# The two ends of a two-model forward pass: inputs in another order, first chunk in halves, last product by token tile

## The reference

```python
for l in range(2):                                   # first block
    proj = rms_norm(h, g_mix[l]) @ w_in[l]            # q, k, v, xr, gr
    o = diff_attention(rope(q), rope(k), v, lam)      # 4 heads of 2 x 64, causal
    y = rg_lru(causal_conv(xr), ...) * gelu(gr)       # lru_lambda -> softplus factors
    h = h + concat([o, y]) @ w_out[l]
    h = h + square(relu(rms_norm(h, g_mlp[l]) @ w_mlp_in[l])) @ w_mlp_out[l]
    gate = sigmoid(rms_norm(h, g_ple[l]) @ w_ple_gate[l])
    h = h + gate * (p[l] @ w_ple_proj[l])
h = rms_norm(h, g_final)
for i in range(4):                                   # second block
    h = h + 0.5 * swiglu(rms_norm(h, norm_ffn1[i]), ...)
    h = h + mixer[i](rms_norm(h, norm_mix[i]))        # stick-breaking, moba, mla, stick-breaking
    h = h + 0.5 * swiglu(rms_norm(h, norm_ffn2[i]), ...)
return rms_norm(h, final_norm)
```

## Time and profile before

| | us |
|---|---|
| median of 3 runs (lowest, highest) | 2667.62 (2664.0, 2668.47) |
| the profiled execution | 2668.11 |
| its span | 2666.3 |
| PE busy | 2598.2 (97%) |
| PE weight loads busy | 2237.3 (84%) |
| DVE busy | 1696.3 (64%) |
| ACT busy | 1348.9 (51%) |
| POOL busy | 57.3 (2%) |

### The profile page before, as it was taken

The page is one execution under the profiler, slowest core; times in us unless marked ns, Lnnn a source line. Parts: engine busy times, 40 slices in busy tenths (PEclk is TensorE's granted clock), DMA queues, the critical chain, the costliest instruction groups (busy, mean ns, idle before and its releaser), DMA issues.

```text
span 2666.3 us, 38170 instructions
## 1 busy us (share of the span) xinstructions
PE 2598.2 (97%) x14918; PEld 2237.3 (84%) x14918; DVE 1696.3 (64%) x1856; ACT 1348.9 (51%) x1593; POOL 57.3 (2%) x27
## 2 busy tenths in 40 slices
PE   7999999999999999999999999999999999999998
PEld 7788887887888988888888888888878888898887
DVE  7665576655766666666666666666756666665765
ACT  6644465445544454454444544544654454454543
POOL 0000000000000000000000000000000000000000
PEclk9999999999999999999999999999999999999999
DMA  7355543554455335545543455555335555543551
GB/s 274 111 195 192 187 146 116 203 189 178 174 189 180 136 130 200 190 174 190 190 157 127 158 189 189 175 190 187 127 131 192 189 176 190 190 154 111 190 189 63
DMA packets 63352, 454.36 MB, mean 170 GB/s; under 512 B 7072, under 2 KB 7328, under 8 KB 8720
## 3 DMA queue, kind: packets, MB, share of 16 engines
q1 hardware_dynamic: 61920, 448.82, 47.2%
q0 software_dynamic: 896, 3.05, 0.3%
q10 hardware_dynamic: 432, 1.00, 0.1%
HBM read 451.79 MB, written 1.05 MB: 170 GB/s over the span
## 4 chain that ended last, share of the span: by engine, by line
PE 90%; DVE 4%; ACT 4%; issue 1%; DMA 1%; SPq 0%; DVEq 0%; ACTq 0%
PE tb L484 24%; PE tb L482 14%; PE acc L269 10%; PE acc L271 9%; PE acc L270 9%; PE tb L481 3%; PE acc L235 2%; PE acc L237 2%; PE acc L238 2%; DVE w_lo L208 1%; PE acc L783 1%; PE tb L300 1%; PE acc L784 1%; PE acc L785 1%; ACT w_hi L201 1%
## 5 line engine op out<-in xcount | busy, mean ns | idle before, releaser
L208 DVE TENSOR_TENSOR w_lo<-raw,w_hi 128x2048 fp32r<-128x2048 f32 x417 | 955.0, 2293 | 323.4 <-ACT w_hi L201 322.7
L484 PE MATMUL tb<-xT,w_hi 128*128 128x512 f32 x2772 | 987.8, 396 | 0.0
L201 ACT ACTIVATE w_hi<-raw 128x2048 fp32r<-128x2048 f32 x426 | 814.2, 1912 | 323.4 <-PE acc L271 279.2
L482 PE MATMUL tb<-xT,w_lo 128*128 128x256 f32 x3168 | 818.4, 279 | 0.0
L482 PEld LDWEIGHTS tb<-xT,w_lo 128*128 128x128 f32 x3168 | 597.0, 188 | 33.8
L484 PEld LDWEIGHTS tb<-xT,w_hi 128*128 128x128 f32 x2772 | 520.2, 188 | 107.0
L269 PE MATMUL acc<-w_hi,cat 128*128 128x512 f32 x1024 | 403.6, 394 | 11.4 <-DVE cat L1865 7.8
L271 PE MATMUL acc<-w_lo,cat 128*128 128x512 f32 x1024 | 399.9, 391 | 0.0
L270 PE MATMUL acc<-w_hi,cat 128*128 128x512 f32 x1024 | 399.7, 390 | 0.0
L269 PEld LDWEIGHTS acc<-w_hi,cat 128*128 128x128 f32 x1024 | 193.0, 188 | 50.8 <-DVE cat L1865 8.7
L271 PEld LDWEIGHTS acc<-w_lo,cat 128*128 128x128 f32 x1024 | 193.0, 188 | 41.1
(11 more groups left out here) (337 smaller groups left out, 3080.0 us busy)
## 6 DMA issues: line engine op xcount, KB each, us to landing
raw<-in_stream SPq DMA_DIRECT2D x426, 1024.0 KB, 4.8
h<-in_x SPq DMA_DIRECT2D x2, 512.0 KB, 4.6
gain<-in_gains POOLq DMA_DIRECT2D x2, 512.0 KB, 9.4
xn<-in_gates POOLq DMA_DIRECT2D x2, 512.0 KB, 8.1
out<-xn SPq DMA_DIRECT2D x2, 512.0 KB, 2.7
cst<-in_consts ACTq DMA_DIRECT2D x1, 832.5 KB, 12.3
big<-in_pT POOLq DMA_DIRECT2D x2, 256.0 KB, 5.5
big<-in_lam_qk POOLq DMA_DIRECT2D x1, 256.0 KB, 10.7
```

The lines of the kernel that those rows point to most:

```text
L201: act.activation(w_hi[:, k % SPLIT, :], raw[:, k % RAW, :], ACT.Copy).then_inc(hi_done, 1)
L208: dve.tensor_tensor(w_lo[:, k % SPLIT, :], raw[:, k % RAW, :], w_hi[:, k % SPLIT, :], ALU.subtract).then_inc(lo_done, 1)
L482: last = pe.matmul(banks[f][:, 0:SEQ], lo, xT[:, kt, 0, :], start=False, stop=False)
L484: last = pe.matmul(banks[f], hi, both, start=False, stop=kt == KT - 1)
```

## The change

**Loads.** The identity now has the column of frequencies beside it (129 columns); the other constants go from ACT's queue to SP's, behind chunk 1. Chunk 0 comes as two halves. POOL's queue brings the positions first, and `lru_par` and `lam_qk` after chunk 1 has landed; the `gain` load stands at the second ple phase. **First chunk.** ACT and DVE split chunk 0 in halves between the pieces of `xT`; PE starts X0 after the first half. Chunk 3 is split before the norm's factor. `start_dve` is divided in `start_angles` (after the remainder of chunk 1), `start_dots` and `start_factors` (ahead of the rotary tables); `start_act` moves behind `rb` and chunk 4. **Spread.** The spread of the factor stands in G0, at step 8 in layer 0 and 2 in layer 1, and not at step 7 of X1. **Gated projections.** The table and the four sigmoids stand ahead of the last weight copy. **End.** The last product finishes token tile 0 first, the factor is made for each tile, POOL multiplies by the gain, and ACT and DVE apply the factor. Shapes and sums are else the same.

```diff
+        def half_hi(act, j):
+
+            act.wait_ge(*(when("half_in", 0) if j == 0 else (raw_full[0], 16)))
+            p = slice(j * HALF, (j + 1) * HALF)
+            act.activation(w_hi[:, 0, p], raw[:, 0, p], ACT.Copy).then_inc(*(sig("half_hi", 0) if j == 0 else (hi_done, 1)))
+
+        def half_lo(dve, j):
+            dve.wait_ge(*(when("half_hi", 0) if j == 0 else (hi_done, 1)))
+            p = slice(j * HALF, (j + 1) * HALF)
+            dve.tensor_tensor(w_lo[:, 0, p], raw[:, 0, p], w_hi[:, 0, p],
+                              ALU.subtract).then_inc(*(sig("half_lo", 0) if j == 0 else (lo_done, 1)))
...
-            pe.wait_ge(lo_done, c + 1 + RAW * i)
+            if c == 0:
+                pe.wait_ge(*when("half_lo", 0))
+            else:
+                pe.wait_ge(lo_done, c + 1 + RAW * i)
...
-            elif acc_done is not None:
+            elif acc_done is not None and not by_tile:
...
+                if kt == KT // 2 and n == 0:
+                    pe.wait_ge(lo_done, 1)
...
-            residual(dve, n, c + CHUNKS_FFN - 1, row_scale)
+            if f < 2 * DEPTH_B - 1:
+                residual(dve, n, c + CHUNKS_FFN - 1, row_scale)
+            else:
+                end_dve(dve, n, c + CHUNKS_FFN - 1)
+
+        END = N_NORMS - 1
...
+        def end_dve(dve, n, c_last):
+
+            def add(t, nn):
+                if (t, nn) == (1, 1):
+                    used(dve, c_last)
+                else:
+                    dve.wait_ge(*when("acc_done", (c_last, t, nn)))
...
+            add(0, 0)
+            add(0, 1)
+            add(1, 0)
+            mean(0)
+            add(1, 1)
+            factor(0)
+            mean(1)
+            factor(1)
+            dve.wait_ge(*when("end_gained", (1, 0)))
+            dve.tensor_scalar(xn[:, 1, 0:512], xn[:, 1, 0:512], e_rstd[:, 1:2], None, ALU.mult).then_inc(*sig("end_half", 0))
+
+        def end_act(act):
+            for t in range(TT):
+                for nn in range(2):
+                    h_ready(act, END, t, nn)
+                    part = slice(nn * 512, (nn + 1) * 512)
+                    last = act.activation(cut(D * t + 512 * nn, 512), h[:, t, part], ACT.Square,
+                                          accum_out=e_ss[:, 2 * t + nn:2 * t + nn + 1])
+                last.then_inc(*sig("sumsq", (END, t)))
+                if t == 0:
+                    act.preload_act_table_set("sqrt_and_others")
+                act.wait_ge(*when("meansq", (END, t)))
+                act.activation(e_rms[:, t:t + 1], e_ms[:, t:t + 1], ACT.Sqrt).then_inc(*sig("root", (END, t)))
+            for t in range(TT):
+                act.wait_ge(*when("end_rstd", t))
+                act.wait_ge(*when("end_gained", (t, 1)))
+                part = slice(0, D) if t == 0 else slice(512, D)
+                act.activation(xn[:, t, part], xn[:, t, part], ACT.Copy, scale=e_rstd[:, t:t + 1])\
+                   .then_inc(*sig("normed", (t, 1)))
+
+        def end_pool(pool):
+            pool.wait_ge(*when("gain_in", END))
+            for t in range(TT):
+                for nn in range(2):
+                    part = slice(nn * 512, (nn + 1) * 512)
+                    h_ready(pool, END, t, nn)
+                    pool.tensor_tensor(xn[:, t, part], h[:, t, part], gain[:, part], ALU.mult).then_inc(*sig("end_gained", (t, nn)))
...
-            for j in range(4):
+            for j in range(3):
                 split_hi(act, c, j + SPLIT)
+            act.preload_act_table_set("sigmoid_and_others")
...
+            split_hi(act, c, 3 + SPLIT)
...
-            product(X1, {7: lambda: spread(pe, n)})
-            product(G0)
+            product(X1)
+            product(G0, {8 if l == 0 else 2: lambda: spread(pe, n)})
...
-            split_hi(act, c, X0 + SPLIT)
+            if l:
+                split_hi(act, c, X0 + SPLIT)
             spread_act(act, n, "mix_a")
             split_hi(act, c, X1 + SPLIT)
+            if l == 0:
+                start_act(act)
             split_hi(act, c, G0 + SPLIT)
...
+            act.wait_ge(*when("factors", 0))
...
-            split_lo(dve, c, X0 + SPLIT)
+            if l:
+                split_lo(dve, c, X0 + SPLIT)
...
+            if l == 0:
+                start_factors(dve)
+                dve.wait_ge(*when("sines", 0))
             dve.tensor_tensor(rb_cos, rb, ropeA[:, 0, :], ALU.mult)
...
+        def start_dots(dve):
+            own = in_turn(dve, "dots")
+            dve.wait_ge(*when("start_in", 1))
             dve.wait_ge(*when("gain_T_in", 0))
...
+        def start_angles(dve):
+            own = in_turn(dve, "angles")
+            dve.wait_ge(*when("places_in", 0))
+            dve.wait_ge(*when("ident_in", 0))
...
-            for k in range(RAW):
+            sp.dma_start(raw[:, 0, 0:HALF], stream[0, :, 0:HALF]).then_inc(*sig("half_in", 0, 16))
+            sp.dma_start(raw[:, 0, HALF:CH], stream[0, :, HALF:CH]).then_inc(raw_full[0], 16)
+            load(1, 1)
+            sp.dma_start(cst[:, C_ROT:C_END], consts[:, C_ROT:C_END]).then_inc(*sig("const_in", 0, 16))
+            for k in range(2, RAW):
...
-                sp.wait_ge(*when("normed", (N_NORMS - 1, t)))
+                sp.wait_ge(*when("normed", (t, 1)))
+                if t:
+                    sp.wait_ge(*when("end_half", 0))
...
+            pool.dma_start(ropeA[:, 1, :].bitcast(mybir.dt.int32), positions.partition_broadcast(P)).then_inc(*sig("places_in", 0, 16))
+            pool.wait_ge(raw_full[1], 16)
             pool.dma_start(lru_par[:, :, :], lru_cols).then_inc(*sig("start_in", 0, 16))
-            pool.dma_start(ropeA[:, 1, :].bitcast(mybir.dt.int32), positions.partition_broadcast(P)).then_inc(*sig("start_in", 1, 16))
-            pool.dma_start(cut(0, 512), lam_qk.partition_broadcast(P)).then_inc(*sig("start_in", 2, 16))
-            pool.dma_start(gain[:, :], gains[0, :].partition_broadcast(P)).then_inc(*sig("gain_in", BRIDGE, 16))
+            pool.dma_start(cut(0, 512), lam_qk.partition_broadcast(P)).then_inc(*sig("start_in", 1, 16))
...
+                    if l == DEPTH_A - 1:
+                        pool.dma_start(gain[:, :], gains[0, :].partition_broadcast(P)).then_inc(*sig("gain_in", BRIDGE, 16))
...
+                if kind == "end":
+                    end_pool(pool)
...
-            act.dma_start(cst[:, 0:P], consts[:, 0:P]).then_inc(*sig("ident_in", 0, 16))
+            act.dma_start(cst[:, 0:C_ROT], consts[:, 0:C_ROT]).then_inc(*sig("ident_in", 0, 16))
             act.dma_start(gain_T[:, :, :], gains_T).then_inc(*sig("gain_T_in", 0, 16))
-            act.dma_start(cst[:, P:C_END], consts[:, P:C_END]).then_inc(*sig("const_in", 0, 16))
+            act.preload_act_table_set("sqrt_and_others")
             act.wait_ge(*when("gain_T_in", 0))
             last_kind = None
             for kind, l, c, n in PHASES:
+                if n == 0:
+                    x_high(act, n, 0)
+                    half_hi(act, 0)
+                    x_high(act, n, 1)
+                    x_high(act, n, 2)
+                    half_hi(act, 1)
+                    x_high(act, n, 3)
+                    for k in range(1, SPLIT + 1):
+                        split_hi(act, k)
+                elif kind != "end":
+                    norm_act(act, n)
+                    split_hi(act, c, -1 + SPLIT)
                 if kind != "end":
-                    norm_act(act, n)
-                if n == 0:
-                    for k in range(SPLIT):
-                        split_hi(act, k)
-                else:
-                    split_hi(act, c, -1 + SPLIT)
-                factor_act(act, n)
-                if n == 0:
-                    start_act(act)
+                    factor_act(act, n)
                 if kind not in ("ffn", "mla", "mix_a"):
                     spread_act(act, n, kind)
                 if kind != "end":
                     MIX[kind][1](act, l, c, n)
+                else:
+                    end_act(act)
...
-                    norm_dve(dve, n, last_kind)
                 if n == 0:
-                    for k in range(SPLIT):
-                        split_lo(dve, k)
+                    x_low(dve, n, 0)
+                    half_lo(dve, 0)
+                    x_low(dve, n, 1)
+                    x_low(dve, n, 2)
+                    half_lo(dve, 1)
+                    x_low(dve, n, 3)
+                    split_lo(dve, 1)
+                    start_angles(dve)
+                    split_lo(dve, 2)
+                    split_lo(dve, 3)
...
-                    start_dve(dve)
+                    start_dots(dve)
```

73 lines of the change are left out of this document (44 added, 29 removed).

## The result

| | before | after |
|---|---|---|
| median, us | 2668.05 (2664.0 to 2669.29, 4 runs) | 2649.18 (2645.5 to 2651.33, 4 runs) |
| profiled execution, us | 2668.11 | 2648.8 |
| its span, us | 2666.3 | 2647.0 |

The ratio is 0.9931, 95% interval 0.9919 to 0.9942: 18.9 us less, where 20.0 had been summed up.

What follows compares the result with a forecast made beforehand. TensorE was taken to bound the kernel, with 90% of the chain, so only its waits, low clock and two ends could be won. Start 9.0, spread 0.9, gated projections 7.8 and end 2.3 sum to 20.0: 2647.6 us, range 2643 to 2653.

Steps and rivals of the forecast that it cites:

- Start, 9.0 predicted: Start of the kernel: scores at 53.5 instead of 62.95, 9.5 us, less 0.5 for the exponentials; ends 7 and 11.5.
- The step that failed: Start: at 428 GB/s the first half of chunk 0 is there by about 7.8, so X0 starts at 10.3.
- whichever clock X0 gets, `rb` is there: Start: `spread` meets `diag` near 27.5, so `rb` stands at 28.3 with X0 ending at 16 or 18.5.
- chunk 1 was not in by 13: Start: a named sign that the prediction is wrong, chunk 1 not having landed by 13 us.
- The rival that gave the start 4.6 us less: Start: chunk 1 lands near 16.98 as before, VectorE's whole queue moves by 4.6 us; 2652.2; chance 0.12.
- `start_factors` 1.9: Start: the moved `start_factors` adds 1.9 us to VectorE's queue between the first `take` and the scores.
- Spread in layer 1, 0.9: Layer 1, X1: TensorE's wait of 0.89 for `diag` goes, 0.9 us; none if VectorE's idle time is not enough.
- Gated projections, 3.9 each: Two gated projections: first wait for `h` 0.2 instead of 2.84, 7.8 us in all; bounds 2.6 and 4.2 each.
- The rival "the low clock stays": Gated projections: TensorE still falls to half clock at a pause of about 1.6 us; 2.6 each, 2650.2; chance 0.10.
- The table: Table loads on ScalarE: 1.28 us each; the skill's drain of about 1.38 on top was left out of the sum.
- The end, 2.3 predicted: After the last matmul: 7.9 us to the end of the span instead of 10.2; 2.3 us, 1.5 to 3.0.
- hidden: End: GpSimd's gain products, 1.2 us a half, run behind each addition, the last to 2658.15, and cost nothing.

Runs made afterwards that it cites:

- positions_late: The changed kernel with the broadcast of the positions issued only when the first half of chunk 0 is in; 2648.68 us.

## Why the prediction was right, term by term

The sum was 20.0 and came out at 19.3 by the spans; the predicted 2647.6 lies 1.6 us under the median of 2649.18. Three of its four terms were near, the one for the end was not. Part of the agreement is luck: the terms as measured below add to 18.7, 0.5 more was gained behind the first attention, most of it at a wait of 1.58 instead of 1.96 whose cause is open, and the low clock at unchanged waits took 0.75 and gave 0.85.

- **Start, 9.0 predicted, 8.3 measured.** At the scores it was 8.5 where 9.5 had been worked out; the 0.5 that was taken off for the exponentials is 0.2 (the wait for them is 0.94, it was 0.74). X0's start was 1.7 us off: the first half of chunk 0 landed at 9.59 and not at 7.8. The step that failed took the rate of another stretch, 428 GB/s, for the microseconds in which the broadcast of the positions was being written; that broadcast is 1.04 of it, and for the other 0.7 no run names a cause. It cost little: `rb` came at 29.08 where 28.3 was expected, and X0 one microsecond earlier gained 0.15 at the scores, since the low pace lasted to 16.7 with the same number of matmuls done. That `spread` and `diag` meet was right (28.34 and 28.29, where 27.5 and 27.4 had been worked out). But "whichever clock X0 gets, `rb` is there" holds only for a microsecond or so of X0: with the whole first chunk, 3.7 us later at X0 is 3.6 us later at the scores. VectorE was late as well: its remainder of chunk 1 starts at 15.62 and not at 14.3, since ScalarE's row stands behind the late first half. That chunk 1 was not in by 13 had been named as a sign of being wrong; ScalarE came to it at 13.64 and did not wait, so this cost nothing.
- **Loads beside the stream.** The rival that gave the start 4.6 us less is what the loads beside the stream measured when they were put back: 4.15. It fell, as the argument against it (x came at full rate) had it, and its size was near. `lam_qk` landed 6.8 us after its issue, long before it was wanted.
- **`start_factors` 1.9, VectorE without a gap from `take` on, the two engines meeting at the scores.** 1.8, no idle time, and a wait of 0.47: as predicted, 0.9 later in all.
- **Spread in layer 1, 0.9.** The wait is gone, and 1.15 with it.
- **Gated projections, 3.9 each.** 4.1 and 3.9. The two waits were called at 0.2 and 1.6, and are 0.15 and 1.56 at the first, 0.15 and 1.94 at the second, where GpSimd's product lengthened an addition by 0.4. The step on the clock (no fall with a short wait) held in all traces. What the prediction took as a fixed part of the old order, the low clock behind the wait (the 1.3 between its 3.9 and its bound of 2.6), is a matter of chance: behind the same wait of 2.84 us the clock fell at once in two cases of four. The rival "the low clock stays" fell.
- **The table.** The sum took 1.28 and no drain for a load; the Trainium skill's "ScalarE: Activation LUTs", What ACT_TABLE_LOAD costs, counts some 1.38 more. In the changed kernel the load at 320.30, straight behind a copy, is followed by the sigmoid at 321.59: the trace doesn't agree, no row shows a drain.
- **The end, 2.3 predicted, 1.3 measured.** This is the term that was mis-sized. Its working set GpSimd's products down as "hidden", since no one waits for them. They were (the last ended at 2640.26, before its scaling), but VectorE stood for 1.1 us in a step of 0.16 while the last one ran. With that product gone the end is 2.4 us shorter than before (10.2 to 7.8), near the sum's 2.3.

What stays open: whether it is the inputs of a VectorE step that decide if GpSimd holds it up, as the two cases suggest; what held back the first half of chunk 0 by the other 0.7 us; and when the clock falls behind a wait of 2 to 3 us, since the same wait gave both.

## What to carry to other kernels

Where TensorE bounds a kernel, look for the engine work that stands between it and its next operand in another engine's queue, and put the work that is wanted later behind it. The edit costs nothing as long as that work has slack, and it pays again wherever the same phase recurs. A wait of TensorE can cost more than its length, by the low clock behind it, so look at the spacing of the matmuls that follow. Where the wait can't be removed, matmuls into a free bank kept the clock up here (4.2 us at two places, a fifth of what the whole change gave). And before a load, a product or a broadcast is called free, look at what runs beside it: the stream's rate, and VectorE's steps.

## What was not expected of the hardware

- TensorE's pace behind a wait of 3.9 us: 0.427 us for a matmul of 512 columns instead of 0.23, for 2 to 6 us, longer in some traces than in others. In the kernel with these gaps filled the mean granted clock was 0.999, and 0.994 in the changed kernel; its five runs lie 3.5 us apart, the four of the changed kernel 5.8. Whether the one makes the other is not shown.
- The clock column can read 1.00 while the matmuls run at the spacing of the low level (positions_late, 10.92 to 16.64): the spacing is the better witness.
- VectorE's product of one column took 1.25 us instead of 0.16 while GpSimd multiplied 128x512 tiles, and ended with it, in nine traces of nine; an addition of 128x512 took 1.08 instead of 0.69 beside a product of GpSimd.
- With a broadcast of 128 KB on GpSimd's queue the DMA engines moved 339 and 80 GB/s in two microseconds that had 303 and 213 without it, of some 425 elsewhere; with the broadcast issued at 8.8 (it landed at 15.3), a dip to 218 stood in 13 to 14, where `lru_par` and `lam_qk` had been issued too.
